# RWKV core of a two-layer trunk: across products of levels 2 to 5 as 32x32 blocks, first chunk's operands prepared beside R's products

## The chip, the cores and the metric

The kernel runs on one core of a Trainium2 chip, in float32 with the large weight products split into float16 parts. The metric is the device time of one execution in microseconds. The kernel before took 2242.28 us, the median of 3 runs (2241.21 to 2245.89).

## What is computed

A trunk of two layers; each has a token mixer between two SwiGLU halves. The first mixer is RWKV-7 time mixing, and its recurrence is the part at hand. Per head (16 heads of 64) a 64x64 state S goes through 528 positions:

```
def step(S, inp):
    r_t, w_t, k_t, v_t, a_t, b_t = inp
    sa = jnp.einsum('bhij,bhj->bhi', S, a_t)
    S = S * w_t[:, :, None, :] + sa[..., None] * b_t[:, :, None, :] + v_t[..., None] * k_t[:, :, None, :]
    return S, jnp.einsum('bhij,bhj->bhi', S, r_t)
```

with w = exp(-exp(w_log)), a = -kk and b = kk * a of the rates. Everything else (norms, products with weights, sliding-window attention in layer two) is the same before and after.

## The kernel before

The program is written engine by engine: each engine has its own list in program order, and semaphores tie the lists together. Nothing is reordered by a scheduler. `Steps` names the counts of one semaphore; `after(e, s, name, i)` waits for step `name` of chunk i.

The function `rwkv` first makes K, V, the rates and R (`r_pe`, `r_act`, `r_dve`). In R's part TensorE runs four pairs of weight tiles in two column halves (L289), and after each half-tile one small product that spreads norms over heads (L313). VectorE's `rates(k)` (L1436, L1440, L1442) make kk, k and b of feature tile k; its `evict` (L1130) takes R's tiles from PSUM; ScalarE's `factor(k)` (L1429) comes before `rates`.

Then `core` runs the recurrence as 9 chunks of 64 positions (528 padded to 576), all 16 heads at once, as 8 pairs of heads on 128 partitions. Half f of a product is 4 pairs, that is 8 heads. In a chunk:

- ScalarE takes `decays` (dec = exp of the summed rates, L1793) and `inverses` (inv, L1798). VectorE multiplies them into operands (L1862): `bn` and `kt` from inv, `al` and `rt` from dec, and copies the last decay (`dl`, L1874).
- TensorE makes scores (L1647): A from bn, K from kt, against [al, rt]. VectorE masks them (L1879) into `bs` and `ks`.
- The chunk needs the inverse of a unit lower triangular 64x64 matrix per head. It is grown by levels: level 1 gives 2x2 blocks, level 6 the whole 64. GpSimd makes the start XT (mask L1951, plus identity L1953) and the level masks N2 to N5 of the scores (L1956, 4 of them). VectorE transposes the start (L1885). For each level l, `up` on TensorE multiplies N_l by X to U, ScalarE copies U out of PSUM (L1805), `across` multiplies U by XT to T, VectorE adds T to XT (L1895) and transposes (L1897) for the next level. Both products of levels 2 to 5 are 64x64 per head (L1656, 8 matmuls per half). Level 6 is `corner`: 32x32 matmuls (L1671 up, L1668 across), with small copies (L1808) and sums (L1902). Chunk 0 has levels 2 to 4 only, since 48 of its positions are padding.
- Between these stand the products of the chunk before (SA, S, Y), three turns of operands by a unit matrix (L1680), the next chunk's scores, and R (the right-hand side). ScalarE copies SA, Y and R (L1815) and the turned operands (L1820); VectorE updates the state (L1908, L1911).

TensorE's order in chunk n is: up 2, across 2, SA of n-1, up 3, S of n-1, across 3, Y of n-1, up 4, two turns, scores A of n+1, across 4, a turn, up 5, scores K of n+1, across 5, R, up 6, across 6. Both halves of a product write banks 0 and 1 (U) and 2 and 3 (T), 256 columns of 512.

A float32 matmul shows as two records of LDWEIGHTS and MATMUL in the trace. The half products of one group thus have 16 records, both halves 32.

## Time and profile before

| | |
|---|---|
| median of 3 runs | 2242.28 us |
| the profiled execution's own time | 2239.5 us |
| its span, first to last instruction | 2237.7 us |
| granted TensorE clock, mean | 0.986 |
| TensorE matmul busy | 2133.5 us, 95% |
| VectorE, ScalarE, GpSimd busy | 1088.0, 803.4, 472.1 us |
| core stage, first score to last Y | 592.6 to 815.9 us |

In the rows below, times count from the span's start in microseconds. A row of the timeline gives start, length of the group from its first start to its last end, engine, line, operation, output<-inputs, shapes and the number of records, and in brackets the engine's idle time before it with what ended it. Adjacent records of one kind are merged into one row, and a window cuts a group at its borders. "x" is the buffer of the normed activations, "cumsum_buf" and "split" hold XT, X, N and U. A row of the stages gives the stretch, its length, the busy time and the number of instructions of each engine, the granted clock (1.00 is 2.4 GHz, 0.50 is 1.2 GHz), the DMA share and GB/s. The end of a matmul is modelled: consecutive records overlap, so paces are read from starts.

### The profile page before, as it was taken

The page shows a single profiled execution, that of the slowest core. Times are in us where ns is not written, and L with a number is a line of the kernel's source. Part 1 is how long each engine was busy: PE and PEld are TensorE (multiplying, and loading weights), DVE is VectorE, ACT ScalarE, POOL GpSimd, SP SyncE. Part 2 cuts the span into 40 slices and gives each one's busy share as a digit, 9 for nine tenths or more (in the row PEclk, how much of TensorE's full clock was granted, in tenths as well). Part 3 has the DMA queues.
Part 4 walks back from the last instruction along what each step waited for, and adds up shares of the span by engine and source line. Part 5 has one row for each costly group of instructions (what it writes and reads, how often), then busy time and mean ns, then how long its engine had stood idle before and what let it go on. Part 6 is the DMA issues. An engine that isn't in the chain of part 4 may idle for free.

```text
span 2237.7 us, 50972 instructions
## 1 busy us (share of the span) xinstructions
PE 2133.5 (95%) x22780; PEld 1843.0 (82%) x22780; DVE 1088.0 (49%) x1546; ACT 803.4 (36%) x1389; POOL 472.1 (21%) x599
## 2 busy tenths in 40 slices
PE   7999999999899998999999999999999779999997
PEld 6888887777699976788888888888887567888886
DVE  5433324767566656843342463333274648433323
ACT  5333322566233352533332253333132435433310
POOL 2111102440142224511111221110134215111112
PEclk9999999999999999999999999999999899999999
DMA  4322321320000022233332132232214012332311
GB/s 163 133 95 102 130 90 38 125 78 20 13 4 5 4 78 77 81 115 107 107 130 83 46 107 102 95 116 106 81 57 122 1 39 76 115 112 102 130 53 39
DMA packets 29100, 183.43 MB, mean 82 GB/s; under 512 B 3233, under 2 KB 8161, under 8 KB 9937
## 3 DMA queue, kind: packets, MB, share of 16 engines
q1 hardware_dynamic: 28032, 178.79, 22.8%
q8 instruction: 180, 2.95, 0.5%
q0 software_dynamic: 848, 1.37, 0.3%
q14 instruction: 40, 0.32, 0.0%
HBM read 174.31 MB, written 4.30 MB: 80 GB/s over the span
## 4 chain that ended last, share of the span: by engine, by line
PE 82%; DVE 11%; ACT 4%; issue 2%; POOL 1%; DMA 0%; SPq 0%; POOLq 0%; DVEq 0%; ACTq 0%
PE psum L289 68%; PE psum L1656 6%; DVE arena L357 2%; DVE arena L405 1%; PE psum L1647 1%; PE psum L383 1%; PE psum L1680 1%; ACT arena L2562 1%; DVE arena L395 1%; POOL arena L480 1%; PE psum L2364 1%; DVE split L264 1%; DVE arena L2603 1%; DVE arena L331 0%; DVE h L362 0%
## 5 line engine op out<-in xcount | busy, mean ns | idle before, releaser
L289 PE MATMUL psum<-x,split 128*128 128x256 f16 (+1 forms) x5568 | 636.1, 275 | 8.6 <-POOL x L424 7.1
L289 PEld LDWEIGHTS psum<-x,split 128*128 128x128 f16 x5568 | 542.2, 98 | 98.3 <-issue 14.1
L289 PE MATMUL psum<-x,split_more 128*128 128x256 f16 (+1 forms) x2496 | 285.3, 275 | 4.4 <-POOL x L424 2.8
L739 POOL TENSOR_TENSOR arena<-arena 128x256 f16<-128x256 f32 (+1 forms) x176 | 120.6, 685 | 786.8 <-ACT arena L576 786.8
L289 PE MATMUL psum<-x,arena 128*128 128x256 f16 (+2 forms) x2448 | 282.0, 276 | 4.7 <-POOL x L991 3.1
L289 PEld LDWEIGHTS psum<-x,split_more 128*128 128x128 f16 x2496 | 243.6, 98 | 40.7 <-issue 3.6
L289 PEld LDWEIGHTS psum<-x,arena 128*128 128x128 f16 (+1 forms) x2448 | 239.9, 98 | 41.6 <-POOL x L991 5.4
L264 DVE SCALAR_TENSOR_TENSOR split<-stage,split 128x2048 f16<-128x2048 f32 (+1 forms) x77 | 189.8, 2466 | 157.5 <-ACT split L258 157.5
L289 PE MATMUL psum<-arena,split 128*128 128x256 f16 (+1 forms) x2304 | 260.9, 275 | 0.0
L289 PEld LDWEIGHTS psum<-arena,split 128*128 128x128 f16 x2304 | 225.1, 98 | 34.5 <-issue 2.2
L659 DVE SCALAR_TENSOR_TENSOR arena<-psum,arena 128x256 f32<-128x256 f32 (+1 forms) x176 | 75.5, 429 | 311.8 <-ACT arena L570 307.2
L570 ACT ACTIVATE arena<-psum 128x256 f32<-128x256 f32 (+1 forms) x176 | 68.3, 388 | 371.9 <-PE psum L289 371.9
L469 ACT ACTIVATE arena<-arena 128x272 f32<-128x272 f32 (+1 forms) x96 | 38.8, 419 | 359.5 <-DVE arena L456 339.6
L258 ACT ACTIVATE split<-stage 128x2048 f16<-128x2048 f32 (+1 forms) x77 | 156.2, 2028 | 27.1 <-PE psum L289 25.5
L456 DVE TENSOR_SCALAR arena<-psum 128x272 f32<-128x272 f32 (+1 forms) x80 | 33.3, 428 | 249.6 <-PE psum L289 249.6
L576 ACT ACTIVATE arena<-arena 128x256 f16<-128x256 f32 (+1 forms) x176 | 74.1, 421 | 195.4 <-DVE arena L664 195.4
L289 PE MATMUL psum<-arena,split_more 128*128 128x256 f16 (+3 forms) x1248 | 143.5, 275 | 0.3
L480 POOL TENSOR_TENSOR arena<-arena 128x272 f32<-128x272 f32 (+1 forms) x84 | 65.9, 784 | 348.6 <-ACT arena L469 345.4
L289 PEld LDWEIGHTS psum<-arena,split_more 128*128 128x128 f16 (+1 forms) x1248 | 121.2, 98 | 21.2 <-issue 2.6
L289 PE MATMUL psum<-arena 128*128 128x256 f16 (+2 forms) x1200 | 136.7, 275 | 0.0
L289 PEld LDWEIGHTS psum<-arena 128*128 128x128 f16 (+1 forms) x1200 | 117.8, 98 | 16.9 <-POOL arena L1012 0.3
L264 DVE SCALAR_TENSOR_TENSOR split_more<-stage,split_more 128x2048 f16<-128x2048 f32 (+2 forms) x36 | 88.8, 2466 | 80.6 <-ACT split_more L258 80.6
(220 smaller groups left out, 2522.4 us busy)
## 6 DMA issues: line engine op xcount, KB each, us to landing
stage<-in_w_gu SPq DMA_DIRECT2D x88, 1024.0 KB, 4.9
stage<-in_w_down SPq DMA_DIRECT2D x32, 1408.0 KB, 6.1
stage<-in_w_rkv SPq DMA_DIRECT2D x12, 1024.0 KB, 4.9
stage<-in_w_out SPq DMA_DIRECT2D x4, 1024.0 KB, 5.1
stage<-in_w_q SPq DMA_DIRECT2D x4, 1024.0 KB, 4.8
stage<-in_w_o SPq DMA_DIRECT2D x4, 1024.0 KB, 5.9
h_spill<-h SPq DMA_DIRECT2D x1, 2112.0 KB, 12.1
out<-h SPq DMA_DIRECT2D x8, 256.0 KB, 2.1
```

Source lines behind the costliest of these rows:

```text
L258: act.activation(job.split[:, 0, 0:job.cols], stage[:, job.u, 0:job.cols], ACT.Copy, scale=W_SCALE).then_inc(w_hi, 1)
L264: dve.scalar_tensor_tensor(out=job.split[:, 1, 0:job.cols], in0=stage[:, job.u, 0:job.cols], scalar=W_SCALE, in1=job.split[:, 0, 0:job.col ...
L289: last = pe.matmul(o, wt(wp, k), xs(xp, k), start=(k == 0 and wp == 0 and xp == 0), stop=(k == tiles - 1 and wp == 1))
L357: dve.scalar_tensor_tensor(out=tmp[:, k % 4, 0:n], in0=mix_out[:, k, a:a + n], scalar=v("gain", T.post_gain + k), in1=rinv[:, a:a + n], op ...
L456: ins = dve.tensor_scalar(mix_out[:, m, a:a + n], bank(i, z)[:, 0:n], 1.0 / W_SCALE, None, ALU.mult)
L469: act.activation(osq[:, q % 2, 0:n], mix_out[:, m, a:a + n], ACT.Square).then_inc(out_sq, 1)
L480: pool.tensor_tensor(ssum[:, a:a + n], ssum[:, a:a + n], osq[:, q % 2, 0:n], ALU.add).then_inc(out_add, 1)
L570: e.activation(gate_s[:, no % 2, 0:n], bank(i)[:, 0:n], ACT.Sigmoid, scale=1.0 / W_SCALE).then_inc(gate_act, 1)
L576: e.activation(hid[s][:, 0, m, 0:n], hid32[:, no % 2, 0:n], ACT.Copy).then_inc(hid_hi, 1)
L659: e.scalar_tensor_tensor(out=gate_x[:, no % 2, 0:n], in0=bank(i)[:, 0:n], scalar=1.0 / W_SCALE ** 2, in1=gate_s[:, no % 2, 0:n], op0=ALU.m ...
L739: e.tensor_tensor(hid[s][:, 1, m, 0:n], hid32[:, no % 2, 0:n], hid[s][:, 0, m, 0:n], ALU.subtract).then_inc(hid_lo, 1)
L1656: last = e.matmul(o[p0:p0 + HD, q], a[p0:p0 + HD, 4 * f + q, 0:CH], b[p0:p0 + HD, 4 * f + q, 0:CH], start=(z == 0), stop=(z == len(terms) ...
```

## The change

Three edits in `core`, and one call in `r_dve`:

1. `across` of levels 2 to 5 calls the new function `blocks`. It issues only the 32x32 blocks on the diagonal of T (16 matmuls per half in place of 8), on row groups at partitions 0, 32, 64 and 96, each writing the same 32 PSUM partitions of the T bank. The rest of the lower 256 columns of the T banks has to be zero: VectorE clears it once, after R's last tile is out. Level 6's across product writes the upper 256 columns. `up` stays at 64x64.
2. The first chunk's inv, bn and kt are made in `first_operands`, which VectorE runs before R's last eviction. `dec` and `inv` move from the activations' buffer to free columns of split_more. ScalarE loads the exponential's table directly after its last factor, and takes inv before dec; it makes inv of chunk 1 before the levels of chunk 0, and in later chunks inverses(m) stands behind level 2's copies and decays(m) behind level 3's (the other way round before).
3. In chunk 0 VectorE itself makes XT (mask and identity), between A's masks and K's; K's masks stand behind level 2's sum, and bn and kt of chunk 1 stand before it. GpSimd starts with N2. The transposes of the start have a semaphore of their own.

```
-                evict(e, r_at[3, 1], 3, 1, r_all)
+                chunks.first_operands(e)
+                evict(e, r_at[3, 1], 3, 1, r_all)
...
+                def blocks(o, f, a, b):
+                    for q in range(4):
+                        for p0 in range(0, P, 32):
+                            r, t = slice(p0, p0 + 32), slice(p0 % HD, p0 % HD + 32)
+                            last = e.matmul(o[r, q, t], a[r, 4 * f + q, t], b[r, 4 * f + q, t], start=True, stop=True)
+                    return last
...
+                        e.wait_ge(s_init, 3)
                         if l < 6:
-                            last = product(bank("T", f), f, (U, XT[n % 2]))
+                            last = blocks(bank("T", f), f, U, XT[n % 2])
                         else:
-                            last = corner(bank("T", f), f, True, X[n % 2], XT[n % 2], first(bs[n % 2]))
+                            last = corner(upper("T", f), f, True, X[n % 2], XT[n % 2], first(bs[n % 2]))
...
+            def first_operands(e):
+                e.memset(dec[:, :, 0:1], 1.0).then_inc(s_init, 1)
+                e.wait_ge(d_dve.sem, d_dve.count(f"b{KT - 1}"))
+                for n, dst, src_ in (("bn", bn[0], b_all), ("kt", kt[0], k_all)):
+                    after(e, o_act, "inv", 0)
+                    e.tensor_tensor(dst, chunk(src_, 0), inv[:, :, :], ALU.mult).then_inc(o_dve.sem, o_dve.step(n))
```

VectorE at the hand-over, from the last rate step (L1442) to the operands of chunk 0. Before:

```order
L1442 SCALAR_TENSOR_TENSOR arena<-arena 128x528 [waits kk_dve]
L1130 TENSOR_SCALAR arena<-psum 128x2x256 [waits step_products]
L1916 MEMSET split 128x512 [waits kk_dve]
L1917 MEMSET x16 128x8
L1862 TENSOR_TENSOR x16<-arena,x16 128x512 [waits operands_act,core_constants]
L1862 TENSOR_TENSOR x16<-arena,x16 128x512 [waits operands_act]
L1862 TENSOR_TENSOR x16<-arena,x16 128x8x64 [waits operands_act] x2
L1874 COPY cumsum_buf<-x16 128x8
```

and now:

```order
L1442 SCALAR_TENSOR_TENSOR arena<-arena 128x528 [waits kk_dve]
L1971 MEMSET split_more 128x8
L1975 TENSOR_TENSOR split_more<-arena,split_more 128x512 [waits operands_act,kk_dve]
L1975 TENSOR_TENSOR split_more<-arena,split_more 128x512 [waits operands_act]
L1130 TENSOR_SCALAR arena<-psum 128x2x256 [waits step_products]
L1878 TENSOR_TENSOR x16<-arena,split_more 128x8x64 [waits operands_act] x2
L1890 COPY cumsum_buf<-split_more 128x8
L1939 MEMSET split 128x512
L1941 MEMSET psum 128x2x256 [waits banks_freed]
```

The two operands of inv now stand before R's eviction (L1130), the memsets behind all operands, and a memset of PSUM is new.

VectorE in chunk 0, from the first masks of scores to the operands of chunk 1 and level 3's first sum. Before:

```order
L1879 TENSOR_TENSOR stage<-psum,cst 128x512 [waits scores_ready_pe] x4
L1885 STREAM_TRANSPOSE split<-cumsum_buf 128x256 [waits start_pool]
L1885 STREAM_TRANSPOSE split<-cumsum_buf 128x256
L1895 TENSOR_TENSOR cumsum_buf<-cumsum_buf,psum 128x256 [waits levels_pe]
L1897 STREAM_TRANSPOSE split<-cumsum_buf 128x256 [waits levels_dve]
L1895 TENSOR_TENSOR cumsum_buf<-cumsum_buf,psum 128x256 [waits levels_pe]
L1897 STREAM_TRANSPOSE split<-cumsum_buf 128x256 [waits levels_dve]
L1862 TENSOR_TENSOR split_more<-arena,x16 128x512 [waits operands_act] x2
L1895 TENSOR_TENSOR cumsum_buf<-cumsum_buf,psum 128x256 [waits levels_pe]
```

and now:

```order
L1895 TENSOR_TENSOR stage<-psum,cst 128x512 [waits scores_ready_pe] x2
L1903 TENSOR_TENSOR cumsum_buf<-stage,cst 128x512 [waits start_dve]
L1905 TENSOR_TENSOR cumsum_buf<-cumsum_buf,cst 128x512 [waits first_inverse_dve]
L1908 STREAM_TRANSPOSE split<-cumsum_buf 128x256 [waits first_inverse_dve]
L1908 STREAM_TRANSPOSE split<-cumsum_buf 128x256
L1878 TENSOR_TENSOR x16<-arena,split_more 128x512 [waits operands_act] x2
L1918 TENSOR_TENSOR cumsum_buf<-cumsum_buf,psum 128x256 [waits levels_pe]
L1920 STREAM_TRANSPOSE split<-cumsum_buf 128x256 [waits levels_dve]
L1918 TENSOR_TENSOR cumsum_buf<-cumsum_buf,psum 128x256 [waits levels_pe]
L1920 STREAM_TRANSPOSE split<-cumsum_buf 128x256 [waits levels_dve]
L1895 TENSOR_TENSOR stage<-psum,cst 128x512 [waits scores_ready_pe] x2
L1918 TENSOR_TENSOR cumsum_buf<-cumsum_buf,psum 128x256 [waits levels_pe]
```

The start of the inverse (L1903, L1905) is VectorE's own and comes before the second pair of masks, and chunk 1's two operands come before level 2's sum (L1895 before, L1918 after), K's masks behind it.

ScalarE from the last factors (L1429) to the copies of chunk 0's levels. Before:

```order
L1429 ACTIVATE split_more<-arena,ka1,vec 128x528 [waits kk_dve] x6
L243 ACT_TABLE_LOAD [waits kk_dve,cumulated_decays]
L243 ACTIVATE eps<-eps 128x1 [waits step_products]
L1793 ACTIVATE x16<-arena 128x8x64
L1798 ACTIVATE x16<-arena 128x512
L1805 ACTIVATE split<-psum 128x256 [waits levels_pe] x2
L1793 ACTIVATE x16<-arena 128x8x64 [waits operands_dve]
```

and now:

```order
L1429 ACTIVATE split_more<-arena,ka1,vec 128x528 [waits kk_dve] x6
L243 ACT_TABLE_LOAD
L243 ACTIVATE eps<-eps 128x1
L1814 ACTIVATE split_more<-arena 128x512 [waits core_constants,cumulated_decays]
L1809 ACTIVATE split_more<-arena 128x8x64
L1814 ACTIVATE split_more<-arena 128x512 [waits operands_dve]
L1821 ACTIVATE split<-psum 128x256 [waits levels_pe] x4
```

The table load no longer waits for the rates and R; inv comes first, and chunk 1's inv before the copies (L1805 before, L1821 after).

TensorE at level 2 of chunk 0, from the second half of the up product to level 3's up product; every later chunk has the same pieces. Before:

```order
L1656 MATMUL psum<-split 64x64 [waits start_pool,start_dve]
L1656 MATMUL psum<-split 64x64 x7
L1656 MATMUL psum<-cumsum_buf,split 64x64 [waits levels_act]
L1656 MATMUL psum<-cumsum_buf,split 64x64 x7
L1656 MATMUL psum<-cumsum_buf,split 64x64 [waits levels_act]
L1656 MATMUL psum<-cumsum_buf,split 64x64 x7
L1656 MATMUL psum<-split 64x64 [waits start_pool,levels_dve]
```

and now:

```order
L1663 MATMUL psum<-split 64x64 [waits start_pool,inverse_start_dve]
L1663 MATMUL psum<-split 64x64 x7
L1673 MATMUL psum<-cumsum_buf,split 32x32 [waits core_constants,levels_act]
L1673 MATMUL psum<-cumsum_buf,split 32x32 x15
L1673 MATMUL psum<-cumsum_buf,split 32x32 [waits core_constants,levels_act]
L1673 MATMUL psum<-cumsum_buf,split 32x32 x15
L1663 MATMUL psum<-split 64x64 [waits start_pool,levels_dve]
```

Each half of the across product goes from 8 matmuls to 16 smaller ones; the products around it stay.

## Rows read from the trace of the kernel before

**Rows 1.** The page: the chain that ended last, by engine.

```profile
PE 82%; DVE 11%; ACT 4%; issue 2%; POOL 1%; DMA 0%; SPq 0%; POOLq 0%; DVEq 0%; ACTq 0%
```

**Rows 2.** The timeline: the hand-over from R's products to the scores.

```profile
585.11 2.79 PE L289 MATMUL psum<-x,split 128*128 128x256 f16 x24
...
586.51 0.70 DVE L1442 SCALAR_TENSOR_TENSOR arena<-arena 128x528 f32<-128x528 f32 x1
...
587.31 1.28 ACT L243 ACT_TABLE_LOAD   x1 [7.64 <-DVE arena L1442]
...
587.94 0.69 DVE L1130 TENSOR_SCALAR arena<-psum 128x512 f32<-128x512 f32 x1 [0.72 <-PE psum L289]
...
589.24 0.61 ACT L1798 ACTIVATE x<-arena 128x512 f32<-128x512 f32 x1
...
589.95 2.50 DVE L1862 TENSOR_TENSOR x<-arena,x 128x512 f32<-128x512 f32 x4 [0.76 <-ACT x L1798]
...
592.59 5.22 PE L1647 MATMUL psum<-x 64*64 64x128 f32 x64 [4.69 <-DVE cumsum_buf L1874]
```

**Rows 3.** Stages of 3.4 us: busy time per engine, granted clock.

```profile
592.30:595.70 3.40, 3.11 (x30) 3.14 (x32) 0.92 (x3) 0.00 (x0) 0.00 (x0) 0.50 0.00 0
...
599.10:602.50 3.40, 1.64 (x48) 1.53 (x50) 0.77 (x2) 0.84 (x3) 3.40 (x4) 1.00 0.02 5
...
602.50:605.90 3.40, 3.27 (x64) 3.08 (x60) 1.69 (x4) 0.99 (x3) 1.89 (x2) 0.51 0.00 0
```

**Rows 4.** The timeline: masks, first inverse and level 2 of chunk 0.

```profile
596.10 0.69 DVE L1879 TENSOR_TENSOR stage<-psum,cst 128x512 f32<-128x512 f32 x1 [0.81 <-PE psum L1647]
...
596.87 1.27 POOL L1951 TENSOR_TENSOR cumsum_buf<-stage,cst 128x512 f32<-128x512 f32 x1 [10.63 <-DVE stage L1879]
...
598.22 1.26 POOL L1953 TENSOR_TENSOR cumsum_buf<-cumsum_buf,cst 128x512 f32<-128x512 f32 x1
...
599.44 4.94 POOL L1956 TENSOR_TENSOR split<-stage,cst 128x512 f32<-128x512 f32 x4
...
599.52 0.77 DVE L1885 STREAM_TRANSPOSE split<-cumsum_buf 128x256 f32<-128x256 f32 x2 [0.98 <-POOL cumsum_buf L1953]
...
600.85 1.15 PE L1656 MATMUL psum<-split 64*64 64x64 f32 x32 [3.04 <-POOL split L1956]
```

**Rows 5.** The timeline: levels 3 and 4 of chunk 0.

```profile
603.71 1.98 PE L1656 MATMUL psum<-split 64*64 64x64 f32 x32
...
606.67 1.29 DVE L1862 TENSOR_TENSOR split_more<-arena,x 128x512 f32<-128x512 f32 x2 [2.15 <-ACT x L1798]
...
608.83 1.90 PE L1656 MATMUL psum<-split 64*64 64x64 f32 x32 [1.98 <-DVE split L1897]
```

**Rows 6.** A steady chunk as a stage, and its level 2 on the timeline.

```profile
669.60:693.80 24.20, 23.58 (x741) 22.92 (x738) 14.90 (x36) 9.18 (x23) 7.46 (x6) 1.00 0.02 4
...
668.92 1.15 PE L1656 MATMUL psum<-split 64*64 64x64 f32 x32
...
669.65 0.85 ACT L1805 ACTIVATE split<-psum 128x256 f32<-128x256 f32 x2 [1.15 <-PE psum L1656]
...
670.09 1.15 PE L1656 MATMUL psum<-cumsum_buf,split 64*64 64x64 f32 x32
```

**Rows 7.** TensorE's timeline: into level 6's corner products and out of them.

```profile
690.98 0.22 PE L1656 MATMUL psum<-stage 64*64 64x64 f32 x1
...
691.13 0.69 PE L1671 MATMUL psum<-split,stage 32*32 32x32 f32 x32
...
693.07 0.19 PE L1668 MATMUL psum<-cumsum_buf,split 32*32 32x32 f32 x1
...
693.19 0.39 PE L1656 MATMUL psum<-split 64*64 64x64 f32 x6
```

**Rows 8.** VectorE's timeline: A's second mask and level 4's first sum.

```profile
683.59 0.69 DVE L1879 TENSOR_TENSOR stage<-psum,cst 128x512 f32<-128x512 f32 x1 [0.18 <-PE psum L1647]
...
684.19 0.41 DVE L1895 TENSOR_TENSOR cumsum_buf<-cumsum_buf,psum 128x256 f32<-128x256 f32 x1
```

More of the change, by code:

```diff
@@ L1821, in turned @@
                         l_act.sem, l_act.step(name) + (SKIP_ACT if (name, n) == ("Kt", 0) else 0))
-                e.wait_ge(done, r_end + 1)
+                warm(e, ACT.Exp)
                 e.wait_ge(c_scan, KT)
-                e.wait_ge(d_dve.sem, d_dve.count(f"b{KT - 1}"))
-                warm(e, ACT.Exp)
+                e.wait_ge(s_init, 1)
+                inverses(0)
                 decays(0)
-                inverses(0)
+                inverses(1)
                 for n in range(NRC):
@@ L1831, in act @@
                     copy_u(2, n)
-                    if m < NRC:
-                        decays(m)
+                    if n and m < NRC:
+                        inverses(m)
                     if i >= 0:
@@ L1837, in act @@
                     if m < NRC:
-                        inverses(m)
+                        decays(m)
                     if i >= 0:
@@ L1882, in start @@
                 def start(m):
-                    e.wait_ge(i_pool.sem, i_pool.count("XT", m))
+                    if m:
+                        e.wait_ge(i_pool.sem, i_pool.count("XT", m))
+                    else:
+                        e.wait_ge(i_dve.sem, i_dve.count("A1", 0))
+                        e.tensor_tensor(XT[0][:, :, :], first(bs[0]), wide("m1T", PAIRS), ALU.mult).then_inc(x_first, 1)
+                        e.wait_ge(x_first, 1)
+                        e.tensor_tensor(XT[0][:, :, :], XT[0][:, :, :], wide("eye", PAIRS), ALU.add).then_inc(x_first, 1)
+                        e.wait_ge(x_first, 2)
                     for f in range(2):
-                        e.transpose(hf2(X[m % 2], f), hf2(XT[m % 2], f)).then_inc(i_dve.sem, i_dve.step(f"X{f}"))
+                        e.transpose(hf2(X[m % 2], f), hf2(XT[m % 2], f)).then_inc(x_dve2.sem, x_dve2.step(f"X{f}"))
                 def grow(l, n):
@@ L1901, in grow @@
                                 x = xt[p0:p0 + 32, :, 32:64]
-                                ins = e.tensor_tensor(x, x, bank("T", f)[p0:p0 + 32, :, 32:64], ALU.add)
+                                ins = e.tensor_tensor(x, x, upper("T", f)[p0:p0 + 32, :, 32:64], ALU.add)
                             ins.then_inc(l_dve.sem, l_dve.step(f"T{l}_{f}"))
@@ L1956, in pool @@
                         e.tensor_tensor(Nk[l][:, :, :], nt, wide(f"m{l}T", PAIRS), ALU.mult).then_inc(
-                            i_pool.sem, i_pool.step(f"N{l}"))
+                            i_pool.sem, i_pool.step(f"N{l}") + (2 if (l, m) == (2, 0) else 0))
             def outputs_ready(e):
                 e.wait_ge(s_act.sem, s_act.count("Y1", LAST))
-            return Part(scalar=act, vector=dve, tensor=pe, gpsimd=pool, ready=outputs_ready)
+            part = Part(scalar=act, vector=dve, tensor=pe, gpsimd=pool, ready=outputs_ready)
+            part.first_operands = first_operands
+            return part
         def epilogue(s_g2, y_done):
```

42 lines of the change are left out of this document (24 added, 18 removed).

## Prediction

> **What bounds the kernel now.** The chain that ended last is 82% TensorE over the whole program [rows 1], so a stage is worth what it costs on TensorE's own path, or what TensorE waits for in it. I read the change's stage in three looks: the hand-over from R's products to the first chunk, the first chunk, and one steady chunk.
>
> Hand-over [rows 2]. R's last products run from 585.11 to 587.90. VectorE ends the last rate step (L1442) at 587.21, ScalarE only then loads the exponential's table (1.28 us), takes two exponentials, and VectorE makes four operands of the chunk in 2.50 us. TensorE begins the scores at 592.59, 4.69 us after it stopped, and the granted clock is 0.50 for the next 3.4 us, 1.2 GHz [rows 3]. 64 score records take 5.22 us.
>
> First chunk [rows 4, 5]. VectorE masks A and then K, GpSimd builds the first inverse in two steps, masks level 2 after that, and the level products start at 600.85, 3.04 us after the scores ended. Level 3's sum (L1895) stands on VectorE behind two operands of chunk 1 which wait 2.15 us for an exponential that ScalarE has put behind level 3's copies. Level 4's products start at 608.83, after another 1.98 us of idle time.
>
> Steady chunk [rows 6]. In 24.20 us TensorE is busy for 23.58, at full clock. What idle time there is lies around level 6, and that chain (corner products and four small ScalarE copies) is not touched. So here only less TensorE work, or an earlier end of it, counts.
>
> **The start, step by step.** All of it is against the profiled execution (span 2237.7, its own time 2239.5 us; the median of the runs shown is 2242.28, so I take the difference off that).
>
> Table load: now behind ScalarE's last factor, where the row shows 7.64 us of idle time [rows 2], so it is hidden. The first exponential waits for the memset of `dec`, which stands behind VectorE's last rate step: 587.3. It takes 0.61 and ends at 587.9. `bn` and `kt` follow on VectorE, 2.50 / 4 = 0.62 each, to 589.2; then the eviction of R's last tile (0.69), which used to stand before them and loses 1.2 us, but nothing except `rt` waits for it; then `al` and `rt` to 591.1. Scores A of chunk 0 start at 591.1 in place of 592.6: **1.5 us** earlier. Behind them stand a small copy, the memset of the state (an old one, 128x512) and the new memset of two PSUM banks, as many elements; no row in the groups has the new one. A mask of as many elements takes 0.69 [rows 4] and bounds it above, below it can't go under nothing; I take 0.5 each. They end at 592.2, as the first half of the scores does, so they cost 0 (bounds 0 and 0.4).
>
> Clock: 32 score records took 592.59 to 596.10 less the wait, 3.5 us, at 1.2 GHz; the same kind at full clock take half. TensorE's pause shrinks from 4.69 to 3.2 us. The nearest row is the pause of 3.04 us before 600.85: the products after it began at full clock (1.00 up to 602.5) and fell to 0.51 only behind that [rows 3, 4]. I take the first half of scores A at full clock and the second at half: 2.6 us in place of 3.5, **0.9 us** (bounds 0 and 1.75).
>
> First inverse: from the end of A's second mask (596.10 + 0.69 = 596.79) to level 2's products 4.06 us passed: GpSimd 1.27 + 1.26, then its level-2 mask 1.23, with the transposes of 0.77 beside it [rows 4]. Now VectorE does mask and sum in 0.69 each (as the row of A's mask), half of the transposes in 0.39, and four hand-overs of 0.05 to 0.08 (as 596.79 to 596.87) add 0.2: 1.97; GpSimd's level-2 mask of 1.27 lies beside it. K's masks, which stood between, are behind. **2.1 us**. The level products of chunk 0 thus start at 596.4 in place of 600.85.
>
> Order within chunk 0: before, from the start of level 2's products to that of level 4's are 608.83 - 600.85 = 7.98 us. Now the operands of chunk 1 stand before level 2's sum, 1.3 us of VectorE while it would have idled until level 2's products were done (1.6 us after their start), because their exponential was taken before. K's two masks (1.3 us) take their place behind level 2's sum, and end 4.6 us after the start; level 3's product, by way of the copies and with level 3's first product still at half clock (1.98 us, [rows 5]), is ready at 4.8. Sum (0.41, [rows 8]), half of the transposes (0.39) and two hand-overs give 5.75. **2.2 us**. If K's masks came last, it would be 0.2 less.
>
> Sum of the start: 1.5 + 0.9 + 2.1 + 2.2 = 6.7, and 0.2 for chunk 0's fourth level (below) = 6.9 us.
>
> **The level products.** 35 products are touched (levels 2 to 4 in nine chunks, level 5 in eight). One was 16 matmuls of 64x64, 32 records, 0.93 us from first to last start (1.15 less 0.22 [rows 6]), with two row groups at work. It becomes 32 matmuls of 32x32, 64 records, on four row groups. The only 32x32 rows are level 6's corners, on two row groups: 32 records in 0.69 - 0.19 = 0.50 us, 16 ns each [rows 7]. If each row group keeps that pace, four of them issue 64 records in the same 0.50 us, 8 ns each; if only two can be at work, it is 1.01 us. Bounds 0.50 and 1.01; I take 0.50, since the two groups there run beside each other at half the time per record of one, and nothing in the row shows a common limit. The TensorE page of the Trainium skill ("TensorE: Matmul & The Clock Gate", Back-to-back issue gap) has a floor of about 25 ns between starts however small the matmul: by it the product would be 64 x 25 = 1.6 us, an estimate. This case's 16 ns in the corners lies under that floor, so I don't use it.
>
> Each of these products now also changes the shape to 32x32 and back. From the last 64x64 start at 690.98 to the first 32x32 start at 691.13 are 0.15 us, back from 693.07 to 693.19 are 0.12, where the mean pace is 0.03 and 0.016; with the slower first records after it (0.05) I put **0.25 us** on the pair of changes. So a product where TensorE is the bound gains 0.93 - 0.50 - 0.25 = 0.18 us.
>
> Per steady chunk. Level 2: the second half can't start before ScalarE's second copy, 669.65 + 0.85 = 670.50 [rows 6]; TensorE leaves level 2 some 0.1 earlier, and VectorE gets the first half 0.24 earlier, which takes away another 0.1 of waiting before level 3. 0.2. Level 3: 0.18. Level 4: VectorE comes to its sum straight from A's second mask, 683.59 + 0.69, with no idle time before 684.19, so a product that is ready earlier finds it busy [rows 8]; 0 (bound 0.18). Level 5: K's masks stand there in the same way, but R's products lie between and TensorE doesn't wait: 0.18. Together 0.56 us, eight chunks: **4.5 us**. Halves of the T banks that stay zero are still read, so VectorE's sums keep their 0.41. Decays and inverses change places on ScalarE; both have over 1 us of slack in a steady chunk, 0.
>
> Sum: 6.9 + 4.5 = 11.4 us. 2242.28 - 11.4 = 2230.9 (the profiled execution: 2228.1). What follows the core has no clock of its own: it waits for Y and shifts with it.
>
> **Rivals.**
> Two row groups at most. The product takes 1.01 + 0.25 = 1.26 us, 0.33 more than before: about 0.2 in level 2 and 0.33 in the others, 1.2 per chunk, 9.6 in eight; the start keeps 6.9 - 0.8 = 6.1. Net +3.5: 2245.8. For it: no row has four groups at work. Against: no sign of a shared limit.
>
> Row groups that write one PSUM bank take turns. Then it is slower: 64 records at a single group's pace, twice 16 ns, are 2.0 us, with the changes 1.35 more than before, 35 times 1.35 = 47, of which some 5 are covered by waits; less 6 of the start: +36, about 2278. The kernel ends slower than before as soon as a product with its shape changes costs more than about 1.15 us, 0.4 above the forecast's 0.75 (11.4 us over the some 29 products that aren't covered). The Trainium skill states this rule ("TensorEngine Tiling (Array Packing)", Gotcha 1: PSUM Pressure: different row tiles can't access the same bank at the same time). Against it, the 64x64 products and the corners here both write one bank from two row groups and keep 16 ns in the corners [rows 7]; they write different partitions.
>
> The start gives less. The clock stays at half for the whole of the scores and of chunk 0's first levels, VectorE's new row of memsets and two sums is late: 4.5 + 2.5 = 7, or half of either part: 2235 to 2238. For it: three stretches at half clock lie in this stage already.
>
> **How the numbers follow.** Forecast 0.71 (2225 to 2236), a weak start or dearer shape changes 0.15 (to 2240), two groups 0.10 (2246), turns on the bank 0.04. The low end has shape changes that cost nothing (5 us more) and no half clock in scores (0.9): 2225 and some; I write 2224. The high end is the weak start, 2240. A measurement here tells about 0.2%, 4.5 us, from no change. Faster: 0.71 + 0.12 of the weak start = 0.83; same: 0.03 of it and 0.09 of two groups = 0.12; slower: 0.01 and 0.04 = 0.05.
>
> **What would show it.** Scores starting near 591 (587.9 + 3.2) and level 2's products 5.3 us after them: start right. Level products at 8 ns a record, 32 records of a half in 0.25 us and steady chunks of 23.6 to 23.8 us in place of 24.27: pace right. 16 ns a record or chunks above 25 us: two groups. 32 ns: turns. VectorE waiting before level 4's sum would say that its masks were not the bound there. Wrong altogether if chunk 0's level 2 still starts 8 us after the scores.

## The result, and the profile of the changed kernel

The changed kernel takes 2256.38 us (median of 4 runs, 2255.58 to 2257.02), the kernel before 2241.78 us (4 runs). The ratio is 1.0061, 95% interval 1.0045 to 1.0077: 14.6 us slower, where 11.4 us faster was forecast. The profiled execution has a span of 2255.0 us against 2237.7, so 17.3 us more; its mean granted clock is 0.983 against 0.986.

The page of the changed kernel, in this order: the span, TensorE's busy time, the instruction queue of the DMA engines, the chain that ended last.

```profile
span 2255.0 us, 53284 instructions
...
PE 2142.1 (95%) x23900; PEld 1841.6 (82%) x23900; DVE 1091.5 (48%) x1549; ACT 803.9 (36%) x1389; POOL 471.5 (21%) x597
...
q8 instruction: 189, 3.10, 0.6%
...
PE 81%; DVE 11%; ACT 3%; issue 3%; POOL 1%; DMA 0%; SPq 0%; POOLq 0%; DVEq 0%; ACTq 0%
```

Against [rows 1] the chain has "issue" at 3% in place of 2%: time in which an engine waited for nothing that the profile shows. The program has 2312 instructions more (before: 50972), and the queue that loads instructions moved 189 packets, 9 more than before.

**Where the time came from.** The core's last copy of Y ends at 833.27 us, before at 816.30: 17.0 of the 17.3 us are there when the core ends. The core started earlier than before: the scores begin at 591.62 (592.59, [rows 2]) and level 2 of chunk 1 is 3.7 us ahead. So the steady chunks lost some 20 us. From one start of level 6's corners to the next they took 25.7, 26.5, 27.7, 27.3, 26.9, 25.8 and 24.7 us, where before they took 24.27 (the first 24.44, the last 20.88).

**What a steady chunk shows.** The same stretch as in [rows 6], as a stage, and TensorE's timeline inside it (start, length, then the group; the bracket is the idle time ahead of it and what ended it):

```profile
669.60:693.80 24.20, 21.78 (x773) 20.34 (x760) 13.63 (x32) 8.15 (x21) 7.45 (x6) 1.00 0.02 4
```

```profile
667.65 1.15 PE L1663 MATMUL psum<-split 64*64 64x64 f32 x32
668.82 0.92 PE L1673 MATMUL psum<-cumsum_buf,split 32*32 32x32 f32 x64
669.67 0.45 PE L1663 MATMUL psum<-split,cumsum_buf 64*64 64x64 f32 x8
670.77 0.86 PE L1663 MATMUL psum<-split,cumsum_buf 64*64 64x64 f32 x23 [0.66 <-issue]
...
678.20 0.21 PE L1663 MATMUL psum<-stage 64*64 64x64 f32 x1 [0.70 <-issue]
...
696.13 1.02 PE L1663 MATMUL psum<-split,cumsum_buf 64*64 64x64 f32 x26
698.05 0.39 PE L1663 MATMUL psum<-split,cumsum_buf 64*64 64x64 f32 x6 [0.90 <-issue]
```

L1663 is `product` (before: L1656), L1673 the new `blocks`. TensorE is busy for 21.78 us of 24.20, before for 23.58. The idle time is new, and it doesn't lie at the semaphores: at 670.77, 678.20 and 698.05 TensorE goes on in the middle of a product, and the releaser is "issue". Most of these stalls lie in 64x64 work that the change did not touch, fewer in the blocks (14 and 5 in the view below). The forecast's product is visible too: 64 records of 32x32 from 668.82 on, of which the first 32 start within 0.26 us.

TensorE's waits by line, from 640 to 790 us (line waited on, releaser: us in total, times, longest):

```profile
PE psum L1663 <- issue: 8.4, 14, 1.0
PE psum L1673 <- issue: 2.9, 5, 1.0
PE psum L1683 <- ACT split L1824: 2.4, 6, 0.4
PE psum L1686 <- issue: 0.3, 1, 0.3
```

The same view of the kernel before has one line. The wait for ScalarE's small copies at level 6 was there already:

```profile
PE psum L1668 <- ACT split L1808: 3.0, 7, 0.4
```

From the starts of all TensorE records (matmuls and weight loads) between 616 and 800 us I counted the gaps of over 0.2 us that end with a record which waits for no semaphore: 24 of them, 16.9 us in sum, and before none. "Stalls" below are these.

**What the stalls stand next to.** TensorE's instructions come from memory in packets of 16 KB on queue q8. Every stall of the changed kernel ends between 1.22 and 1.58 us after such a packet landed: the stall 669.90 to 670.77 after a landing at 669.42, 677.29 to 678.20 after 676.78, 696.94 to 698.05 after 696.68, 725.36 to 726.43 after 724.98. Packets follow each other every 3.9 us, so a link by chance to a window of 0.36 us is not likely over 24 stalls. The place of the stalls in the program says the same without any times: between the ends of two stalls that follow each other stand 250 to 254 TensorE records for each packet that landed meanwhile (250 for one, 506 for two, 757 for three, 1010 for four). So, but for the few of a block's 256 instructions that have no record, the stalls end a whole number of blocks apart, whatever product stands there. A 64x64 matmul of 4-byte numbers here leaves two weight loads and two matmuls in the trace. A steady chunk before had 736 records of each, 1472 instructions; four blocked products add 128 records of each, 256 instructions, one packet per chunk more. The Trainium skill ("Runtime: NRT & Kernel Launch", Instruction fetch mechanics) says that an engine's instruction memory is refilled in blocks of 16 KiB, 256 instructions, which fits these counts (1472 / 256 = 5.75 packets, and 24.27 / 4.17 = 5.8 seen in a chunk, by the landings counted below). It also says that this is mostly hidden. Here it was until the change.

### The profile page after: what moved, and what is told of

Read it like the earlier page. It is cut to its first block, busy times and chain, and to the rows that moved or that the text cites. A ratio compares the mean times of both kernels' runs of the same rounds, so it can differ in the third digit from the quotient of the medians.

```text
span 2255.0 us, 53284 instructions
## 1 busy us (share of the span) xinstructions
PE 2142.1 (95%) x23900; PEld 1841.6 (82%) x23900; DVE 1091.5 (48%) x1549; ACT 803.9 (36%) x1389; POOL 471.5 (21%) x597
## 4 chain that ended last, share of the span: by engine, by line
PE 81%; DVE 11%; ACT 3%; issue 3%; POOL 1%; DMA 0%; SPq 0%; POOLq 0%; DVEq 0%; ACTq 0%
PE psum L289 68%; PE psum L1663 5%; DVE arena L357 2%; PE psum L1654 1%; DVE arena L405 1%; PE psum L383 1%; PE psum L1695 1%; PE psum L1673 1%; ACT arena L2596 1%; DVE arena L395 1%; POOL arena L480 1%; PE psum L2398 1%; DVE split L264 1%; DVE arena L2637 1%; DVE arena L331 0%
## 5 line engine op out<-in xcount | busy, mean ns | idle before, releaser
L258 ACT ACTIVATE split<-stage 128x2048 f16<-128x2048 f32 (+1 forms) x77 | 156.2, 2028 | 26.9 <-PE psum L289 25.5
L289 PEld LDWEIGHTS psum<-arena 128*128 128x128 f16 (+1 forms) x1200 | 117.8, 98 | 16.9 <-POOL arena L1012 0.3
```

Source lines behind the costliest of these rows:

```text
L258: act.activation(job.split[:, 0, 0:job.cols], stage[:, job.u, 0:job.cols], ACT.Copy, scale=W_SCALE).then_inc(w_hi, 1)
L289: last = pe.matmul(o, wt(wp, k), xs(xp, k), start=(k == 0 and wp == 0 and xp == 0), stop=(k == tiles - 1 and wp == 1))
```

## The experiments

All ratios are against the kernel before on the same chip, with 95% intervals. The theories, as the expectations number them: 1, TensorE's instructions come too slowly; 2, the changed start costs time; 3, blocks save what was forecast; 4, changes of shape cost it; 5, four row groups at work bring the stalls; 6, VectorE and GpSimd slow each other in chunk 0.

### The start alone, and the blocks alone

```diff
-                            last = blocks(bank("T", f), f, U, XT[n % 2])
+                            last = product(bank("T", f), f, (U, XT[n % 2]))
```

> The changed kernel with the across products of levels 2 to 5 put back to 64x64; the earlier start stays. Theory 1 (TensorE's instructions come in too slowly: in the changed kernel the 16 KB packets of the instruction queue follow each other every 3.9 us in the core stage and 26 stalls without a semaphore stand inside products): with 64 instructions fewer per level no stalls, steady chunks back to 24.27 us, level 2 of chunk 1 some 3.5 us earlier than before, in all 2238 us, 3.5 under the kernel before. Theory 2 (the earlier start or its moved operands cost the time, the blocks not): still above 2250 us.

2237.65 us (10 runs) against 2241.68: 0.9982 (0.9973 to 0.9992). No stalls, chunks of 24.27 us (one of 24.50). The start gains 4.0 us, not 6.9.

The other half is the kernel before with `blocks`, the two T banks set to zero once, and level 6's products of T in the banks' upper half:

```diff
+                        e.wait_ge(s_init, 3)
...
-                            last = product(bank("T", f), f, (U, XT[n % 2]))
+                            last = blocks(bank("T", f), f, U, XT[n % 2])
```

> The kernel before with nothing but the 32x32 across products, their cleared T banks and level 6 in the upper halves. Theory 1 (instruction supply): chunks of 26 to 27 us after the first two, in all the kernel before plus 17 to 21 us, 2259 to 2263. Theory 2 (the start costs): at most 2243. Theory 3 (the blocks save TensorE time as forecast): 2237.

2257.22 us (4 runs): 1.0070 (1.0053 to 1.0086), 15.5 us slower. Chunks of 25.4 to 26.3 us, 15 stalls of 9.9 us in all; chunks and total are a little under what theory 1 had expected. So the loss is that of the blocks, and theory 2 falls. The two parts sum to +11.5; the changed kernel has +14.6. The 3 us between are within the intervals of the times (up to 3.7 us to either side), but the traces show that the parts don't simply add: the steady chunks are 1.0 us longer in the changed kernel than with the blocks alone (26.7 and 25.7 us in the mean, below).

### Half of the blocks: the shape changes stay, the instructions don't grow

Only the upper 32x32 block of each head is issued, which leaves out half of the level products. There are as many instructions as before, and each product still changes the shape twice.

```diff
-                        for p0 in range(0, P, 32):
+                        for p0 in (0, 64):
```

> The changed kernel with only the upper 32x32 block of each head's across product issued (row groups 0 and 64), the lower block is left out, so the result differs. 16 records per half as before the change, but still a change of shape to 32x32 and back in every level. Theory 1 (instruction supply): no stalls, steady chunks of 23.6 to 23.8 us, in all about 2233 to 2235. Theory 4 (the stalls belong to the changes of shape, or to small products writing a bank beside others): stalls stay, chunks above 25.5 us, 2250 or more.

2234.38 us (6 runs): 0.9967 (0.9955 to 0.9979). TensorE's timeline, two of the products, and the stage of [rows 6]:

```profile
678.13 0.69 PE L1673 MATMUL psum<-cumsum_buf,split 32*32 32x32 f32 x32
682.93 0.69 PE L1673 MATMUL psum<-cumsum_buf,split 32*32 32x32 f32 x32
```

```profile
669.60:693.80 24.20, 23.49 (x759) 22.10 (x756) 14.85 (x35) 9.26 (x23) 7.45 (x6) 1.00 0.02 4
```

A product is 32 records in 0.69 us, like the corners of [rows 7]. Chunks took 23.77 to 24.06 us, with a single stall of 0.23 us. With shape changes but no more instructions the kernel gets faster; theory 4 falls.

### As many instructions as the changed kernel, without the small shape

Each 64x64 product in two halves of 32 columns with the same 64x64 weights, so 64 records as in the blocks:

```diff
-                        for p0 in range(0, P, 32):
-                            r, t = slice(p0, p0 + 32), slice(p0 % HD, p0 % HD + 32)
-                            last = e.matmul(o[r, q, t], a[r, 4 * f + q, t], b[r, 4 * f + q, t], start=True, stop=True)
+                        for t in (slice(0, 32), slice(32, 64)):
+                            for p0 in (0, HD):
+                                r = slice(p0, p0 + HD)
+                                last = e.matmul(o[r, q, t], a[r, 4 * f + q, 0:CH], b[r, 4 * f + q, t],
+                                                start=True, stop=True)
```

> The changed kernel with each across product issued as 64x64 weights against two halves of 32 columns: as many instructions as the changed kernel (32 records per half), no 32x32 shape, nothing on four row groups, and TensorE's own time about that of the 64x64 product (0.93 to 1.01 us). Theory 1 (instruction supply): stalls as in the changed kernel, steady chunks of 26.4 us or more, in all 2255 to 2259. Theory 4 (shape changes or four row groups): no stalls, chunks of 24.3 to 24.6, 2238 to 2241.

2266.44 us (4 runs): 1.0111 (1.0096 to 1.0126), and no stall at all; every steady chunk took 27.65 or 27.7 us. The product on the timeline:

```profile
672.86 2.06 PE L1674 MATMUL psum<-cumsum_buf,split 64*64 64x32 f32 x64
```

64 records in 2.06 us are 29 ns each ((2.06 - 0.22) / 63), the pace of the 64x64 products before, though each moves half the columns. The run was meant to hold TensorE's work and double its instructions; for these products it doubled both. With TensorE slower, 1728 instructions in 27.65 us are 16.0 ns each, as many as before (24.27 us / 1472 = 16.5), and the supply kept up. That is in line with theory 1, but tells nothing apart, and the expectation of stalls was wrong, as was the time (2255 to 2259 expected).

### Four row groups at the number of instructions before

Blocks for two of a half's four pairs of heads, which leaves out half of the level products; all four row groups work as in the changed kernel:

```diff
-                    for q in range(4):
+                    for q in range(2):
```

> The changed kernel with the across blocks of two of four pairs per half only (q in 0 and 1, the other two pairs are left out, so the result differs): four row groups at work and the shape changes as in the changed kernel, but 16 records per half, as many instructions as before the change. Theory 1 (instruction supply): no stalls inside products, steady chunks of 23.3 to 23.7 us, 2231 to 2234 in all. Theory 5 (four row groups at once, not the number of instructions, bring the stalls): stalls stay, at least half of them, chunks above 25 us, 2245 or more.

2229.54 us (3 runs): 0.9953 (0.9936 to 0.9969). The product, the one stall between 616 and 800 us, and the waits from 640 to 790 us:

```profile
678.65 0.46 PE L1673 MATMUL psum<-cumsum_buf,split 32*32 32x32 f32 x32
...
687.62 0.22 PE L1686 MATMUL psum<-split,stage 32*32 32x32 f32 x2 [1.02 <-issue]
```

```profile
PE psum L1683 <- ACT split L1824: 2.8, 7, 0.4
PE psum L1686 <- issue: 1.0, 1, 1.0
```

32 records in 0.46 us are 8 ns each ((0.46 - 0.22) / 31) on four row groups. The chunks took 23.2 to 23.4 us, but for the one with the stall (25.51). The total lies 1.5 us under the range that theory 1 gave, and the one stall was not expected. Four row groups at full pace don't bring the stalls; theory 5 falls.

### All the blocks, two row groups at a time

The upper blocks of the heads, then the lower ones, as many instructions as in the changed kernel:

```diff
-                    for q in range(4):
-                        for p0 in range(0, P, 32):
-                            r, t = slice(p0, p0 + 32), slice(p0 % HD, p0 % HD + 32)
-                            last = e.matmul(o[r, q, t], a[r, 4 * f + q, t], b[r, 4 * f + q, t], start=True, stop=True)
+                    for s0 in (0, 32):
+                        for q in range(4):
+                            for p0 in (s0, s0 + HD):
+                                r, t = slice(p0, p0 + 32), slice(p0 % HD, p0 % HD + 32)
+                                last = e.matmul(o[r, q, t], a[r, 4 * f + q, t], b[r, 4 * f + q, t],
+                                                start=True, stop=True)
```

> The changed kernel with the same blocks in another order: first the upper blocks of all four pairs (row groups 0 and 64), then the lower ones (32 and 96). The same number of instructions, never more than two row groups at work, 16 ns a record, so 1.0 us for a product in place of 0.5. Theory 1 (instruction supply): the chunk is bound by about 6.75 packets of 16 KB at 3.9 us each, so 26 to 27 us as in the changed kernel although TensorE has more work, stalls still there but shorter, 2253 to 2258 in all. Theory 5 (four groups): no stalls, chunks of 25.0 to 25.6 us from TensorE's own work and the shape changes, 2246 to 2250.

2252.42 us (3 runs): 1.0048 (1.0031 to 1.0065), chunks of 25.4 to 26.4 us, 14 stalls of 8.0 us in all. Time and chunks lie between the two expectations or just under theory 1's; what decides is that there are stalls at all. TensorE's waits from 640 to 790 us:

```profile
PE psum L1663 <- issue: 2.7, 7, 0.6
PE psum L1685 <- ACT split L1826: 2.5, 6, 0.4
PE psum L1674 <- issue: 1.6, 4, 0.6
PE psum L1688 <- issue: 0.5, 1, 0.5
PE psum L1654 <- issue: 0.2, 1, 0.2
```

The stalls are there with the groups two by two as well. It is not a pure case: the 64 records of a product start within 0.74 or 0.88 us and not the 1.0 expected, 12 to 14 ns apart in the mean, so lower blocks start beside upper ones in part. But the run above had all four groups at 8 ns a record and one stall. Together, the stalls follow the number of instructions per time and not the row groups.

### One level, two levels

```diff
-                        if l < 6:
+                        if l == 3:
                             last = blocks(bank("T", f), f, U, XT[n % 2])
+                        elif l < 6:
+                            last = product(bank("T", f), f, (U, XT[n % 2]))
```

> The changed kernel with blocks in level 3 alone, 64x64 in levels 2, 4 and 5: 64 LDWEIGHTS and MATMUL more per chunk in place of 256, 6.0 packets of 16 KB. Theory 1: at 3.9 us a packet the supply needs 23.4 us, less than TensorE's work, so no stalls, chunks of 24.1 us (0.18 less), 2236 in all, 1 to 2 under the start alone. Theory 5 (four groups bring stalls): a quarter of the changed kernel's loss, chunks of 24.8, 2241 to 2243.

2237.66 us (10 runs): 0.9988 (0.9978 to 0.9997), 4 stalls of 1.9 us in all, chunks of 24.3 to 25.1. I had expected 24.1 and no stalls: the supply has less room than I thought. The second run has `if l in (3, 5):` in the same place.

> The changed kernel with blocks in levels 3 and 5, 64x64 in 2 and 4: 6.25 packets of 16 KB per chunk. Theory 1: the supply needs 24.4 us at 3.9 a packet, just above TensorE's 23.9, so single stalls, chunks of 24.2 to 24.6, 2237 to 2240 in all: a knee between one and two levels. Theory 5: half of the changed kernel's loss, chunks of 25.4, 2246 or so.

2240.89 us (9 runs): 0.9997 (0.9987 to 1.0006), 8 stalls of 3.4 us in all, chunks of 24.1 to 25.1, a little over what theory 1 had expected. With the same start, none, one, two and four blocked levels give 2237.65, 2237.66, 2240.89 and 2256.38 us (against the kernel before on the same chip -4.0, -3.2, 0.0 and +14.6), and stalls of 0, 1.9, 3.4 and 16.9 us. The first blocked level is worth nothing and the later ones cost more and more.

### Instructions per time, all runs side by side

From the landings of the 16 KB packets between 640 and 765 us (256 instructions each), the mean time between two, and what that is per instruction:

```
kernel              instr./chunk   chunk us      between landings   per instr.   stalls 616-800
before                  1472       24.27         4.17 us (30)       16.3 ns       none
start only              1472       24.27         4.16 us (30)       16.2 ns       none
half of the blocks      1472       23.8 - 24.1   4.09 us (30)       16.0 ns       1,  0.2 us
two pairs of four       1472       23.2 - 23.4   4.07 us (31)       15.9 ns       1,  1.2 us
64x64 split             1728       27.65         4.06 us (30)       15.9 ns       none
level 3 only            1536       24.3 - 25.1   3.99 us (31)       15.6 ns       4,  1.9 us
levels 3 and 5          1600       24.1 - 25.1   3.86 us (32)       15.1 ns       8,  3.4 us
changed kernel          1728       25.7 - 27.7   3.90 us (32)       15.2 ns      24, 16.9 us
blocks only             1728       25.4 - 26.4   3.73 us (33)       14.6 ns      15,  9.9 us
two groups              1728       25.4 - 26.4   3.74 us (34)       14.6 ns      14,  8.0 us
```

The instruction queue in that stretch (queue, kind: packets, MB, share of 16 engines), first the kernel before, then the one with two groups:

```profile
q8 instruction: 30, 0.49, 1.5%
```

```profile
q8 instruction: 34, 0.56, 1.7%
```

At 15.9 ns per instruction and above there is one stall at the most, at 15.6 and below there are 4 to 24, and no kernel got below 14.6 ns on the mean of the stretch. Single packets come faster than that: the shortest time between two landings is 3.2 to 3.4 us in every one of these kernels, the one before too (13 ns per instruction). At 14.6 ns the blocked chunk's 1728 instructions need 25.2 us, whatever TensorE could do with them; the forecast was 23.7. Why the changed kernel has more and longer stalls than the one with blocks only (15.2 against 14.6 ns) no run tells.

### The start: GpSimd beside VectorE

The start gained 4.0 us in place of 6.9, and the timeline of the changed kernel shows VectorE and GpSimd instructions that are longer than their like. This run is the start alone, with GpSimd's level masks of chunk 0 held back until VectorE has made the first inverse:

```diff
+                    if m == 0:
+                        e.wait_ge(x_first, 2)
```

> The start alone (64x64 products) with one more wait: GpSimd's level masks of chunk 0 begin when VectorE has ended the two steps of the first inverse. In the start alone VectorE's second step took 1.64 us and GpSimd's masks 1.70 each while they ran side by side, against 0.69 and 1.27 alone. Theory 6 (VectorE and GpSimd slow each other when both only read and write SBUF): the second step back to 0.69, the first mask near 1.27 to 1.7 (transposes beside it), level 2 starts 2.8 to 2.9 us after A's second mask as with both side by side (2.93), total 2237 to 2238. Rival (the second step is slow by itself, from its own input's wait or the constant it reads): 1.64 stays and level 2 starts 1 us later.

2235.84 us (7 runs): 0.9977 (0.9966 to 0.9988), 1.2 us under the expected range. The last run also puts chunk 1's operands behind level 3's sums:

```diff
-                inverse_operands(1)
...
+                    if n == 0:
+                        inverse_operands(1)
```

> As the one before, and the two operands of chunk 1 (bn, kt) move from ahead of level 2's sum to behind level 3's in chunk 0. In the start alone they took 0.94 and 1.75 us beside GpSimd's masks and level 2's sum began 0.9 us after its product was done. Expected: level 2's sum follows its product at once, level 2 to level 4 of chunk 0 in 5.7 to 5.9 us in place of 6.6, total 0.8 us under the start alone, 2236 to 2237.5, under both kernels. Rival: the operands are now late for the turn and the scores of chunk 1 and the gain is given back there, total as the start alone.

2235.62 us (8 runs): 0.9975 (0.9965 to 0.9985), 0.4 us under the expected range. The rows of chunk 0's first inverse and of level 2's sum, first in the start alone:

```profile
595.75 0.69 DVE L1903 TENSOR_TENSOR cumsum_buf<-stage,cst 128x512 f32<-128x512 f32 x1
595.86 6.73 POOL L1988 TENSOR_TENSOR split<-stage,cst 128x512 f32<-128x512 f32 x4 [7.90 <-DVE stage L1895]
596.47 1.63 DVE L1905 TENSOR_TENSOR cumsum_buf<-cumsum_buf,cst 128x512 f32<-128x512 f32 x1
...
598.84 2.62 DVE L1878 TENSOR_TENSOR x<-arena,split_more 128x512 f32<-128x512 f32 x2
...
601.38 0.41 DVE L1918 TENSOR_TENSOR cumsum_buf<-cumsum_buf,psum 128x256 f32<-128x256 f32 x1
```

then with GpSimd's masks held back:

```profile
595.82 0.69 DVE L1905 TENSOR_TENSOR cumsum_buf<-cumsum_buf,cst 128x512 f32<-128x512 f32 x1
...
596.68 5.85 POOL L1990 TENSOR_TENSOR split<-stage,cst 128x512 f32<-128x512 f32 x4 [9.80 <-DVE cumsum_buf L1905]
597.24 2.93 DVE L1878 TENSOR_TENSOR x<-arena,split_more 128x512 f32<-128x512 f32 x2
598.09 1.15 PE L1663 MATMUL psum<-split 64*64 64x64 f32 x32 [0.78 <-POOL split L1990]
```

and with the operands moved too:

```profile
598.75 4.94 POOL L1991 TENSOR_TENSOR split<-stage,cst 128x512 f32<-128x512 f32 x4 [11.09 <-DVE cumsum_buf L1905]
600.16 1.15 PE L1663 MATMUL psum<-split 64*64 64x64 f32 x32 [0.79 <-POOL split L1991]
...
602.05 0.42 DVE L1918 TENSOR_TENSOR cumsum_buf<-cumsum_buf,psum 128x256 f32<-128x256 f32 x1 [2.66 <-PE psum L1663]
```

The identity's sum (L1905) falls from 1.63 back to 0.69 us once GpSimd stands still. GpSimd's four masks take 6.73 us beside VectorE's two-input instructions, 5.85 with one of the collisions gone, and 4.94 with both gone, as in [rows 4]. From level 2's products to its sum pass 2.74 us in the start alone (598.64 to 601.38) and 1.89 with the operands moved. So theory 6 holds, in the rows. What each step is worth on the path is less plain. With GpSimd held back, level 2's products start 3.03 us after the end of A's second mask, in the start alone 2.93: VectorE's second step is short again, but now GpSimd's mask, which began later, is waited for, as was expected. The gain lies behind it: from level 2's products to level 4's pass 6.62 us in the start alone, 5.88 with GpSimd held back and 5.78 with the operands moved too, and forecast were 5.75. Against the kernel before on the same chip, the last two gain 5.4 and 5.6 us and the start alone 4.0; the differences are within the intervals. Each of the three versions is faster than the kernel before by 4 to 6 us, and which of them is best isn't told.

## Why the prediction was wrong, point by point

**The step that failed: what a level product costs.** It was priced by how fast TensorE starts records, 0.50 us for 64 of them. Their number never entered the sum as a cost: 64 more instructions per product, which something must deliver. The parts of that price, from the gaps between the starts of TensorE's matmul records from 640 to 790 us, divided by the chunks in them:

```
gap between starts      start only   half of the blocks   blocks only   changed kernel
under 60 ns, us/chunk     19.5          17.7                17.6           17.7
60 to 200 ns               3.3           4.3                 4.9            4.7
over 200 ns                1.4           1.7                 3.2            4.4
chunk                     24.3          23.8                25.7           26.7
```

(The number of chunks is that of the matmul records, divided by the 736 or 864 of one chunk.) Right was the pace: the blocks take 1.9 us from the first row, forecast 4 x 0.43 = 1.7. The changes of shape lie in the second row: +1.0 with half of the blocks, 4 x 0.25 as forecast, and 1.4 to 1.6 with all of them, a little dearer. The third row, which holds the stalls and the waits for semaphores, was forecast at nothing. It grows by 1.8 us with the blocks alone and by 3.0 in the changed kernel (of it the stalls are 1.6 and 2.9), while it grows by 0.3 where the instructions stay at 1472. So the forecast of -0.56 us per chunk would have held about where instructions stay (-0.2 to -0.5 with half of the blocks), and was +1.1 to +3.4 with all of them.

Could it have been read before? The rows gave it: 741 matmul and 738 load records in 24.2 us [rows 6] are one instruction per 16.4 ns, and 0.50 us for a product's 128 would be 4 ns each. Asking whether anything in the trace of before sustains more than one instruction per 16 ns was the missing question. No row answered it with yes; that should have been a rival with a chance and not nothing. The 25 ns floor of the Trainium skill ("TensorE: Matmul & The Clock Gate"), which I set aside by the corners' 16 ns, is not what happened either: the blocks start 8 ns apart in the mean. But its direction was right, a cost per instruction however small.

**Rivals.** "Two row groups at most" was wrong by its mechanism (8 ns a record on four groups). "Turns on one PSUM bank" was wrong too: four row groups write one bank at 8 ns a record. Its break-even, a product dearer than 1.15 us, was the right test to set: the true price, with the supply, lay above it (0.93 + 1.5 / 4 = 1.3 us with the blocks alone). "The start gives less" came true in its size, 4.0 in place of 6.9 us, with other reasons (below). The range ended at 2240 and the result lies 16 us outside it, since no rival raised the cost of instructions that TensorE itself runs quickly.

**The start, one by one.** The scores came 3.41 us after R's products ended, forecast 3.2: right; R's end itself moved 0.3 us late, so they came at 591.62. The clock: from the first score to the end of A's second mask are 3.40 us (594.33 + 0.69 less 591.62), forecast 2.6 + 0.69, before 4.20. The number is right, in part by luck. The clock was at half for much of this stage too:

```profile
592.30:595.70 3.40, 3.40 (x40) 3.40 (x38) 2.41 (x4) 0.00 (x0) 0.54 (x1) 0.56 0.00 0
```

And the same stretch of the same instructions took other times in the other runs that have this start, one profiled execution each: 2.69 us in the start alone, 3.1 to 3.5 in three more, and 4.41 in five, where half clock covered all of it. The forecast's bounds for this term, 0 and 1.75 us, hold all of these but for 0.2 us; that its 0.9 fits the execution profiled here is chance.

First inverse: from there to level 2's products 2.93 us, forecast 1.97; the missing 1.0 us is L1905 at 1.64 in place of 0.69. Order in chunk 0: level 2 to level 4 took 6.77 us, before 7.98, forecast 5.75. The missing 1.0 us is VectorE's two operands, priced at 1.3 together while it would have idled, which took 2.62 and held level 2's sum until 600.69; with them moved away it was 5.78. The changed kernel:

```profile
595.16 6.73 POOL L1988 TENSOR_TENSOR split<-stage,cst 128x512 f32<-128x512 f32 x4 [8.60 <-DVE stage L1895]
595.78 1.64 DVE L1905 TENSOR_TENSOR cumsum_buf<-cumsum_buf,cst 128x512 f32<-128x512 f32 x1
...
597.95 1.15 PE L1663 MATMUL psum<-split 64*64 64x64 f32 x32 [0.96 <-DVE split L1908]
598.14 2.62 DVE L1878 TENSOR_TENSOR x<-arena,split_more 128x512 f32<-128x512 f32 x2
...
600.69 0.41 DVE L1918 TENSOR_TENSOR cumsum_buf<-cumsum_buf,psum 128x256 f32<-128x256 f32 x1
```

The steps of 2.1 and 2.2 us both used durations from rows in which GpSimd stood still or VectorE had an instruction of another kind. In [rows 4] VectorE never ran an instruction with two inputs in SBUF beside GpSimd's; the change put them side by side, and both got longer. K's masks did stand beside GpSimd's steps, but read one of their inputs from PSUM, and kept their 0.69 us:

```profile
596.97 0.69 DVE L1879 TENSOR_TENSOR stage<-psum,cst 128x512 f32<-128x512 f32 x1 [0.18 <-PE psum L1647]
```

Summing up: 6.9 less these two, and less the 0.5 us by which the scores came late, is 4.4 us; the start alone measured 4.0 in the median. That these two agree so well is also chance, since the clock's term moves by more. The mechanisms were right, two sizes were off, and the clock's share is not the same in every execution.

**VectorE before level 4's sum** can't be judged in the changed kernel, where the stalls cover it. With half of the blocks, which has hardly any, it was as forecast: A's second mask at 683.05, level 4's sum at 683.66, and no idle time between them.

## What to carry to other kernels

Before small matmuls are multiplied, divide the stage's time by all of TensorE's instructions in it, loads too: at about 16 ns each this stage was near what could be delivered, and saving array time by issuing more and smaller pieces bought nothing here. Idle time with the releaser "issue" in the middle of a product, beside landings of 16 KB instruction packets, is the sign of it. And when an instruction is moved beside another engine's, take its duration from a row where both run.

## What the runs showed of the hardware

- TensorE's instructions arrived at one per 14.6 ns at best over 125 us (a packet of 256 each 3.73 us), though in bursts it ran the 128 of one blocked product in 0.56 us. Stalls end 1.2 to 1.6 us after a packet's landing, and a whole number of 256-instruction blocks apart. Whether the engine waits for the packet itself, or for its sequencer to pass from one block of 256 to the next, was not told apart.
- Records on different row groups start 6 to 7 ns apart, and a row group starts its next one 32 ns after its last, with two groups (7 and 25 ns in turn, 16 in the mean) as with four (7, 7, 7 and 12, 8 in the mean), all into one PSUM bank. The pace follows the weights' shape: 64x64 weights took 29 ns a record with 64 columns moved and with 32.
- Whether the clock is at half when the first scores run differs between executions of the same instructions: first score to the end of A's second mask took 2.69 to 4.41 us.
- A VectorE instruction of two SBUF inputs (128x512, 0.69 us alone) took 1.63 to 1.75 us beside a GpSimd one, and GpSimd's took up to 1.72 in place of 1.27. With one input in PSUM it stayed at 0.69 beside GpSimd (596.97 us, kernel before). The Trainium skill states a lock between the two ("SBUF — State Buffer", SBUF: two separate sides): whoever holds the port pair blocks the other for a whole instruction. The trace agrees: in the changed kernel L1905 began at 595.78, GpSimd's first mask ended at 595.16 + 1.70 = 596.86, and L1905 0.56 us later, near its 0.69 alone.
